# Expert layers in 19 passes of 128 places, in an order made on the chip, summed by one-hot products

## The reference, cut to what matters

```python
e_flat = expert_id.reshape(-1)                     # 512 tokens x 2 experts of one group of 8
order = jnp.argsort(e_flat)                        # assignments sorted by expert, 64 experts
...
def expert_block(args):                            # xb (128, 1024); w1, w3 (1024, 256); w2 (256, 1024)
    xb, e = args
    return (jax.nn.silu(xb @ w1[e]) * (xb @ w3[e])) @ w2[e]
...
out = jnp.zeros((n_tok, dm), h.dtype).at[tok_sorted].add(
    g_sorted[:, None].astype(h.dtype) * y_disp[dest])
```

## Time and profile before

| | |
|---|---|
| median of 3 runs | 1572.75 us (1572.18 to 1574.54) |
| span of the profiled execution | 1571.5 us |
| PE busy | 1344.6 us, 86% |
| DVE busy | 491.8 us, 31% |
| ACT busy | 295.4 us, 19% |
| POOL busy | 290.5 us, 18% |
| DMA | 472.17 MB, mean 300 GB/s |

### The profile page before, as it was taken

The page is one execution under the profiler, slowest core; times in us unless marked ns, Lnnn a source line. Parts: engine busy times, 40 slices in busy tenths (PEclk is TensorE's granted clock), DMA queues, the critical chain, the costliest instruction groups (busy, mean ns, idle before and its releaser), DMA issues.

```text
span 1571.5 us, 19548 instructions
## 1 busy us (share of the span) xinstructions
PE 1344.6 (86%) x6176; PEld 624.6 (40%) x6176; DVE 491.8 (31%) x1034; ACT 295.4 (19%) x584; POOL 290.5 (18%) x412
## 2 busy tenths in 40 slices
PE   7999998987887878878799899999978878878786
PEld 5555463332332323333464565453323323333332
DVE  7996145211111111112605572253111111111114
ACT  6236111110010010101235642111100100101000
POOL 2104002332222222222000000003322222222220
PEclk9999999999899998999799899999999998999999
DMA  5423845999999999999410307049999999999996
GB/s 211 166 103 131 347 176 220 374 393 405 405 397 404 403 396 412 397 401 380 174 54 1 121 1 294 23 172 389 402 394 404 390 392 403 404 411 404 394 397 276
DMA packets 83427, 472.17 MB, mean 300 GB/s; under 512 B 13953, under 2 KB 16145, under 8 KB 32816
## 3 DMA queue, kind: packets, MB, share of 16 engines
q1 hardware_dynamic: 69792, 445.25, 71.7%
q0 software_dynamic: 11568, 19.90, 3.8%
q10 hardware_dynamic: 2016, 6.34, 1.0%
HBM read 453.54 MB, written 27.39 MB: 306 GB/s over the span
## 4 chain that ended last, share of the span: by engine, by line
PE 42%; SPq 35%; DVE 11%; DMA 6%; issue 5%; ACT 1%; DVEq 0%; POOL 0%; ACTq 0%; POOLq 0%
SPq L1744 23%; PE ps L1534 13%; SPq L1749 12%; PE ps L1554 5%; DMA ring<-in_moe_w 4%; PE ps L442 4%; PE ps L885 3%; PE ps L904 2%; PE ps L315 2%; PE ps L908 2%; PE ps L431 2%; PE ps L391 2%; PE ps L1524 1%; DVE extra L549 1%; DVE x L558 1%
## 5 line engine op out<-in xcount | busy, mean ns | idle before, releaser
L1534 PE MATMUL ps<-ring,region_b 128*64 128x512 f32 x1408 | 348.8, 653 | 78.2 <-issue 51.3
L1534 PEld LDWEIGHTS ps<-ring,region_b 128*64 128x64 f32 x1408 | 118.2, 150 | 305.8 <-issue 267.1
L1671 DVE TENSOR_TENSOR extra<-extra,ps 128x256 f32<-128x256 f32 x64 | 26.9, 421 | 579.8 <-ACT extra L1608 544.9
L1534 PE MATMUL ps<-wbuf,region_b 128*64 128x512 f32 x320 | 159.6, 657 | 40.0 <-DMA region_a<-in_moe_w 22.2
L1554 PE MATMUL ps<-ring,extra 128*64 128x512 f32 x704 | 160.8, 598 | 34.0 <-DVE extra L1677 31.7
L1534 PE MATMUL ps<-region_a,region_b 128*64 128x512 f32 x320 | 159.8, 658 | 0.0
L1478 POOL DMA_INDIRECT region_b<-hrow,icol x120 | 111.4, 928 | 147.9 <-issue 147.9
L1608 ACT ACTIVATE extra<-ps 128x256 f32<-128x256 f32 x64 | 24.5, 383 | 585.3 <-PE ps L1534 551.7
L1490 POOL DMA_INDIRECT ytok<-extra,icol x120 | 106.1, 884 | 152.6 <-issue 152.6
L1684 DVE COPY extra<-ps 128x512 f32<-128x512 f32 x64 | 44.3, 692 | 241.7 <-PE ps L1554 241.6
L1534 PEld LDWEIGHTS ps<-wbuf,region_b 128*64 128x64 f32 x320 | 46.6, 150 | 145.7 <-issue 136.9
(11 more groups left out here) (322 smaller groups left out, 1511.8 us busy)
## 6 DMA issues: line engine op xcount, KB each, us to landing
ring<-in_moe_w SPq DMA_DIRECT2D x264, 1024.0 KB
wbuf<-in_moe_w SPq DMA_DIRECT2D x80, 1024.0 KB
region_a<-in_moe_w SPq DMA_DIRECT2D x40, 1024.0 KB
ytok<-ring SPq DMA_DIRECT2D x8, 1024.0 KB, 10.2
wbuf<-in_ev_w_in SPq DMA_DIRECT2D x3, 2048.0 KB, 14.3
wbuf<-in_ev_w_out SPq DMA_DIRECT2D x2, 2048.0 KB, 14.6
hrow<-region_a ACTq DMA_DIRECT2D x8, 512.0 KB, 10.4
region_a<-ytok SPq DMA_DIRECT2D x8, 512.0 KB, 5.0
```

Source lines behind the costliest of these rows:

```text
L1534: last = TE.matmul(ps[CAP * g:CAP * (g + 1), 2 + j, :], xtr[j][:, k, CAP * g:CAP * (g + 1)], up_weights(2 * slot + g, k), start=k == 0, st ...
```

## The change

The 64 experts are put in an order made on the chip. Experts 0 to 5 come first as they are. Of the others, those with more than 32 assignments are put on the eight further wide places, and the rest follows (`turns`). CAP is 32: a block has 128 places and holds either two wide experts of 64 or four of 32 (`strips`). There are 19 blocks or passes, in the order `ORDER`: two, two, four, and then four times two, four, four, four experts. DVE also makes the list `elist` of experts by turn, and SP reads each expert's number from it before it loads its weights. The six slots are now slots of single experts. Each pass has one gather of 128 places.

In a pass of four, up and down products are for four strips of 32 columns. Nothing is scattered: `pick` makes for each pass a one-hot matrix with the gates, and `te_combine` multiplies it with `yo` in eight products of 128 by 128 by 512, which DVE adds into x; `ytok`, its zeros and its read-back are gone. `hid`, `hidT`, `yo` and the up product's bank are there once. The sixth slot's up weights lie in `extra` in place of `region_a`, and all six first experts are loaded ahead of the first up product; what `extra` held in the expert layers is in a new buffer, `scr`. The overflow blocks compute with 32 places for an expert.

```diff
-CAP = 64
-QUART = CAP // 4
+CAP = 32
+ROWS = 4 * CAP
+HEAVY = 8
+STATIC = 6
 OVMAX = 2 * T // CAP - 1
-NBLK = NE + OVMAX + 1
...
+def strips(block):
+    if block < 2:
+        return [(64 * g, 64, 2 * block + g) for g in range(2)]
+    if block < 6:
+        return [(64 * g, 64, 2 * block + 2 + g) for g in range(2)]
+    if block == 6:
+        return [(32 * g, 32, r) for g, r in enumerate((4, 5, 14, 15))]
+    return [(32 * g, 32, 4 * block - 12 + g) for g in range(4)]
+ORDER = [0, 1, 6] + [b for i in range(4) for b in (2 + i, 7 + 3 * i, 8 + 3 * i, 9 + 3 * i)]
+NP = len(ORDER)
+NBLK = NP
+TIMES = [(p, r) for p, b in enumerate(ORDER) for _, _, r in strips(b)]
+WHEN = {r: t for t, (p, r) in enumerate(TIMES)}
+PASS_AT = [p for p, r in TIMES]
...
-            S.wait_ge(s_zf, 128)
+            S.wait_ge(s_wc, 2)
...
+        def places_tensor(l):
+            for i in range(2):
+                TE.wait_ge(s_hot, 2 * l + i + 1)
+                for j in range(8):
+                    last = TE.matmul(ps[:, 6 - i, 0:NBLK], hot_s[:, j, :], hot_v[i][:, j, :], start=j == 0, stop=j == 7)
+                last.then_inc(s_tab, 1)
+            TE.wait_ge(s_ec, l + 1)
+            TE.matmul(ps[0:1, 7, 0:NE], ecol[0:NE, :], ident[0:NE, 0:NE], start=True, stop=True).then_inc(s_er, 1)
...
+            vlink(V.memset(xin[1], 0.0))
...
+            of_choice(rk8, rk.rearrange("p c (g e) -> p c g e", g=NG))
             V.wait_ge(s_rc, 2 * l + 2)
-            ts(quart, cnt, float(QUART), ALU.is_gt)
-            for j in range(2, CAP // QUART):
-                stt(quart, cnt, float(QUART * j), quart, ALU.is_gt, ALU.add)
-            vlink(V.tensor_copy(used[:, :], quart[0:1, :]))
-            turned_ranks(rk)
-            of_choice(destf, place.rearrange("p c (g e) -> p c g e", g=NG))
...
+        def turns(l):
+            late, row, two = (con[:, i:i + NE] for i in (C_LATE, C_ROW, C_WIDE))
+            stt(e1, cnts, CAP + 0.5, late, ALU.is_gt, ALU.mult)
+            vlink(V.tensor_tensor_scan(e2, ones[:, 0:NE], e1, 0.0, ALU.mult, ALU.add))
+            ts(hn, e2[:, NE - 1:NE], -(STATIC - 1.0), ALU.add)
+            stt(e3, e2, 2.0, tcount[:, 0:NE], ALU.mult, ALU.subtract)
+            stt(e3, e3, hn, e1, ALU.subtract, ALU.mult)
+            stt(e1, e2, e2[:, NE - 1:NE], late, ALU.subtract, ALU.mult)
+            tt(e3, e3, e1, ALU.subtract)
+            tt(turn_of, e3, tcount[:, 0:NE], ALU.add)
+            stt(wide, turn_of, STATIC + HEAVY - 0.5, two, ALU.is_lt, ALU.mult)
+            ts(e1, turn_of, float(STATIC + HEAVY), ALU.min, 32.0, ALU.mult)
+            stt(e1, turn_of, 32.0, e1, ALU.mult, ALU.add)
+            ts(e2, turn_of, STATIC + HEAVY - 0.5, ALU.is_gt, 64.0, ALU.mult)
+            tt(e1, e1, e2, ALU.add)
+            tt(e1, e1, row, ALU.add)
+            stt(e1, wide, 8192.0, e1, ALU.mult, ALU.add)
...
+        def places(l):
+            of_choice(code8, by_expert(e1))
+            ts(wide8, code8, 8191.5, ALU.is_gt)
+            stt(over8, wide8, -float(CAP), rk8, ALU.mult, ALU.add)
+            ts(far8, over8, CAP - 0.5, ALU.is_gt, FAR, ALU.mult)
+            stt(dest8, wide8, -8192.0, code8, ALU.mult, ALU.add)
+            tt(dest8, dest8, rk8, ALU.add)
+            tt(dest8, dest8, far8, ALU.add)
+            ts(blk8, dest8, 1.0 / ROWS, ALU.mult, -(ROWS - 1) / (2.0 * ROWS), ALU.add)
+            ts(blk8, blk8, ROUND, ALU.add)
+            ts(blk8, blk8, -ROUND, ALU.add)
+            stt(dest8, blk8, -float(ROWS), dest8, ALU.mult, ALU.add)
+            tt(hot_b, tcount[:, None, 0:NBLK].to_broadcast([P, 8, NBLK]),
+               blk8[:, :, None].to_broadcast([P, 8, NBLK]), ALU.is_equal)
+            tt(hot_v[0], hot_b, con[:, C_ID8:C_ID8 + 8][:, :, None].to_broadcast([P, 8, NBLK]), ALU.mult)
+            V.tensor_tensor(hot_s, tcount[:, None, 0:ROWS].to_broadcast([P, 8, ROWS]),
+                            dest8[:, :, None].to_broadcast([P, 8, ROWS]), ALU.is_equal).then_inc(s_hot, 1)
...
+        def gated_places(l):
+            V.tensor_tensor(hot_v[1], hot_b, g12[:, :, None].to_broadcast([P, 8, NBLK]), ALU.mult).then_inc(s_hot, 1)
+        def expert_list(l):
+            ts(eqt, turn_of[0:NE, :], con[0:NE, C_PIX:C_PIX + 1], ALU.is_equal)
+            tt(eqt, eqt, tcount[0:NE, 0:NE], ALU.mult)
+            V.reduce_sum(ecol[0:NE, :], eqt, AX.X).then_inc(s_ec, 1)
...
+        def tables_vector(l):
+            V.wait_ge(s_tab, 2 * l + 1)
+            V.tensor_scalar(blkidx[:, :], ps[:, 6, 0:NBLK], float(NOROW), None, ALU.add).then_inc(s_dst, 1)
+            ts(tokf, ps[:, 6, 0:NBLK], float(NOROW), ALU.add)
+            V.wait_ge(s_tab, 2 * l + 2)
+            vlink(V.tensor_copy(gatef, ps[:, 5, 0:NBLK]))
+            V.wait_ge(s_er, l + 1)
+            V.tensor_copy(elist[:, :], ps[0:1, 7, 0:NE]).then_inc(s_el, 1)
...
+            V.tensor_scalar(back.rearrange("p c t -> p (c t)"), tcount, tokf[:, b:b + 1], gatef[:, b:b + 1],
+                            ALU.is_equal, ALU.mult).then_inc(s_sel, 1)
...
-        def ex_scatter(l, p, j):
-            G.wait_ge(ml["s_ye"][l], 2 * p + 2)
-            G.sem_inc(s_gate2, 1)
-            glink_at(G.tensor_copy(icol[0:CAP, 4 + 2 * j:6 + 2 * j], blkidx[0:CAP, 1, bass.ds(2 * p, 2)]), s_ic[l][1], p + 1)
-            def rows(g, n):
-                G.indirect_dma_start(ytok[l],
-                                     bass.IndirectOffsetOnAxis(ap=icol[0:n, 4 + 2 * j + g:5 + 2 * j + g], axis=0),
-                                     yo[j][CAP * g:CAP * g + n, :], None, bounds_check=2 * T - 1, oob_is_err=False)\
-                    .then_inc(s_yst[l][j], 16)
-            for g in range(2):
-                quarters(2 * p + g, g, rows)
...
+        def gather(n):
+            l, q = n // NP, n % NP
+            if q > 1:
+                G.wait_ge(s_xtp, 2 * (n - 1))
+            b = ORDER[q]
+            G.indirect_dma_start(xin[q % 2], None, hrow[l], bass.IndirectOffsetOnAxis(ap=blkidx[:, b:b + 1], axis=0),
+                                 bounds_check=T - 1, oob_is_err=False).then_inc(s_xi[q % 2], 16)
+        def moe_gpsimd(l):
+            G.wait_ge(s_hst, 64 * l + 64)
+            G.wait_ge(s_dst, l + 1)
+            for q in range(1, NP):
+                gather(NP * l + q)
+        def te_rows(n):
...
+                for r, t in strip_slots(q):
+                    last = TE.matmul(ps[r, 2, :], xtr[:, k, r], up_weights(t % SLOTS, k),
+                                     start=k == 0, stop=k == KC - 1)
+            last.then_inc(s_up, 1)
...
+        def te_combine(n):
+            TE.wait_ge(s_ye, 2 * n + 2)
+            TE.wait_ge(s_sel, n + 1)
+            for i in range(8):
+                if 8 * n + i > 3:
+                    TE.wait_ge(s_ca, 8 * n + i - 3)
+                TE.matmul(ps[:, SUMS[i % 4], :], back[:, i // 2, :], yo[:, (i % 2) * 512:(i % 2 + 1) * 512],
+                          start=True, stop=True).then_inc(s_cb, 1)
...
+            te_rows(NP * l)
+            places_tensor(l)
+            for q in range(NP):
+                n = NP * l + q
+                te_up(n)
+                if q < NP - 1:
+                    te_rows(n + 1)
+                te_hidden(n)
+                te_down(n)
+                te_combine(n)
+                if q == NP - 2:
+                    extra_tensor(l, overflow(TE, l))
...
+        def added(n, i):
+            V.wait_ge(s_cb, 8 * n + i + 1)
+            xs = x[:, i // 2, (i % 2) * 512:(i % 2 + 1) * 512]
+            V.tensor_tensor(xs, ps[:, SUMS[i % 4], :], xs, ALU.add).then_inc(s_ca, 1)
...
+            SP.wait_ge(s_el, l + 1)
+            for q in range(NP):
+                todo = []
+                for t in range(STATIC, NE):
+                    if PASS_AT[t] == q:
+                        r = TIMES[t][1]
+                        e = SP.value_load(elist[0:1, r:r + 1], min_val=0, max_val=NE - 1)
+                        todo.append((t, e))
+                for t, e in todo:
+                    SP.wait_ge(s_up, NP * l + PASS_AT[t - SLOTS] + 1)
+                    up_weights_load(t % SLOTS, l, e, s_w13[t % SLOTS])
+                for t, e in todo:
+                    SP.wait_ge(s_dn, 2 * (NP * l + PASS_AT[t - SLOTS]) + 2)
+                    down_weights_load(t % SLOTS, l, e, s_w2[t % SLOTS])
...
-        def combine_sync(l):
-            for j in range(2):
-                nc.sync.wait_ge(s_yst[l][j], 8 * NE - 32 * j)
-            for n in range(8):
-                c, k = n // 2, n % 2
-                nc.sync.dma_start(gath[n // 4][:, n % 4, :], ytok[l][k * T + c * P:k * T + (c + 1) * P, :])\
-                    .then_inc(s_gat[c], 16)
...
-            sp.wait_ge(s_wc, 2)
-            for l in range(2):
-                rows_ = ytok[l].rearrange("(a p b) d -> a p (b d)", p=P, b=2)
-                for n in range(4):
-                    sp.dma_start(rows_[n], toep.rearrange("p s n -> p (s n)")).then_inc(s_zf, 16)
...
+            for e in range(4):
+                up_load(0, e)
```

(47 more changed lines are left out.)

818 lines of the change are left out of this document (318 added, 500 removed).

## The result

The changed kernel takes **1526.97 us** (median of 4 runs, 1526.58 to 1527.47) against 1572.47 (4 runs, 1570.88 to 1574.54): ratio 0.971, 95% interval 0.9696 to 0.9724, faster by 45.5 us. The prediction said 1530. The profiled execution has a span of 1524.8 us.

The account below looks back on a forecast made before the run. The weight stream was taken as the bound, with PE waiting. Start 2.7 plus 495.7 gave 498.4 us a layer, saving 23.2 and 18.9: 1571.5 - 42.1 = 1529.4, as a median 1530.7, said as 1530; eight in ten 1504 to 1562.

Parts of the forecast that it names:

- Gathers, 1.5 us a pass: Weight stream in the expert layers: each pass's 128-place gather costs 1.5 us, low end 0.54, high end 1.98.
- goes with DMAs: Stretch of 4 us at 338 GB/s in each old pair: if its loss follows DMA count, 0.93 us a pass.
- goes with rows: The same stretch of slow weight stream: if its loss follows gathered rows, 1.98 us a pass.
- Start, +2.7 us: Routing ahead of each layer's first up product: DVE's new chain makes it 2.7 us later, range 1 to 6.
- 6 us late: Failure sign: the prediction fails if the first up product starts over 6 us late.
- Holes, 5.8 and 7.6 us and 0.8 later: Early passes: DMA idles 5.8, then 7.6 us, as loads wait for up products of passes 1 and 2; 0.8 in pass 5.
- Four strips abreast, 6.9 and 3.65: Four-expert passes: four 32-column strips run side by side, up product 6.9 us, down product 3.65, as for two experts.
- the prediction's 1.3 times: Four-strip products: by the Trainium skill they would cost about 1.3 times what was taken, for a sum of 1548.
- Stream, 421 GB/s: Weight stream in the expert layers: 3 MiB at 421 GB/s, 7.47 us for each of 58 experts.
- The rival of 398: Weight stream stays at 398 GB/s, slowed by the mix with PE's and DVE's reads: 1560 us, chance 0.12.
- One-hot product, 7.1 with additions beneath it: End of each pass: one-hot product takes 7.1 us, eight additions run beneath it, the last ending 0.8 behind.
- Zeros, 0: First mixer: removing the 8 MB of zeros was taken to save 0 us.

Follow-up runs that it names:

- the pair of runs on the kernel before: The kernel before without its scatters, 1550.52 us, and without its row gathers from the third pair on, 1500.47 us, both against 1572.76.
- a_no_early_sums: The changed kernel without the one-hot products and additions of passes 0 and 1 in each layer: 1505.86 us, ratio 0.9571.

## Why the prediction was right, step by step

The size held, and so did the cause: the stream is the bound, and it is shorter by the scatters and by gathers in fewer DMAs. By the runs the scatters were worth 22.2 us, and the gathers' price went from 72.3 to 28.5; the longer starts (13.1) and the holes (some 20) take half of these 66 us back. By its own ledger (1529.4 predicted for the span, 1524.8 measured) errors of opposite sign nearly cancel: the starts came 7.7 us longer in sum, the layers behind them 11.3 shorter. That the number is so close is in part luck.

**Gathers, 1.5 us a pass.** Mis-sized: 1.0. The choice of the middle between "goes with DMAs" (0.93) and "goes with rows" (1.98) was the error; the runs say DMAs. The prediction's working with 1.0 gives 489.2 a layer for its 495.7, 6.5 less. The reading of the earlier trace rows behind it, that the slow stretch is the gather's and not the scatter's, is shown by the pair of runs on the kernel before.

**Start, +2.7 us.** Mis-sized, and the step that failed is the sentence that PE's table products end inside DVE's chain. From the first record of the rows product to the first up product were 12.8 us (234.07 to 246.87), and are now 19.4 (235.77 to 255.16), 19.7 in layer 1: +6.6 (in layer 1, from 13.3, +6.5), past the 6 us late at which the prediction said that it would fail; only the other terms kept the sum. Before, the rows product and the one table, of 16 records:

```profile
234.07 7.03 PE L1280 MATMUL ps<-region_a,extra 128*128 128x512 f32 x16
241.52 1.89 PE L1295 MATMUL ps<-extra 128*64 128x64 f32 x16 [0.41 <-DVE extra L1381]
```

After, DVE's copy of the rows, and the rows product, the tables and the first up product of layer 1:

```profile
249.91 0.67 DVE L1644 COPY region_b<-ps 128x512 f32<-128x512 f32 x1
```

```profile
1013.57 7.03 PE L1316 MATMUL ps<-region_a,region_b 128*128 128x512 f32 x16
...
1026.06 7.01 PE L1325 MATMUL ps<-region_b 128*128 128x19 f32 x32 [3.19 <-DVE region_b L1425]
...
1033.31 9.63 PE L1553 MATMUL ps<-ring,region_b 128*64 128x512 f32 x32
```

DVE's chain was costed well (the copy of the rows is through at 250.6). PE was not: the tables wait for DVE's one-hots until 247.9, and 8 products, 16 records, for each of two tables, at 219 ns a record and the lower clock, end at 254.9. Wide weights against 19 moving columns stood in no row that I had read, and I priced neither the shape nor the clock. The kernel before had the nearest row, its own table at 118 ns a record: at that rate (an estimate) 32 records need 3.8 us, and end at 251.7, behind the copy of the rows too.

**Holes, 5.8 and 7.6 us and 0.8 later.** Measured 10.0 in two holes where they were said to be, and shown to lie on the path by `a_no_early_sums`. Most of the 3.4 us less go with passes 0 and 1, which took 23.0 and 22.1 (255.16 to 278.12 to 300.23) for 24.1 and 24.0: the overflow places fit beneath the one-hot product, and the counts held it up by 1.38 us, not 3.0. Passes that wait for nothing take PE 20.5 (300.23 to 320.71), not 21.1.

**What is left over in the layers.** With gathers at 1.0 and holes of 10.0 the working would come to some 485.8 (an estimate: 489.2 less 3.4). The profile has 491.7 and 488.4, so 5.9 and 2.6 us are losses that no term held. In layer 0, 2.2 are in the tail: from the last up product to the last addition 25.9 (720.96 to 746.87) for 23.75, where DVE works on the next norm between additions. About 1.0 is POOL's loads of router weights, named above. The rest is in part a late hole, which both layers have in the last group of passes. In layer 1:

```profile
1440.00:1450.00 10.00, 10.00 (x70) 3.49 (x62) 0.78 (x2) 0.52 (x2) 0.00 (x0) 0.77 0.83 342
```

```profile
1448.94 0.81 SPq L1696 DMA_DIRECT2D wbuf<-in_moe_w  x2
```

SP issues the next loads right behind the up product of that pass, which began after a wait of 3.65 us, took 9.96 and ended at 1448.73: (422 - 342)/422 x 10 = 1.9 us lost. In layer 0 the same pass's product took 9.77, and 670 to 680 ran at 389 GB/s. No run shows what these dips cost by themselves, and what is left beside them stays open.

**Four strips abreast, 6.9 and 3.65.** Held: 7.07 to 7.09 at the full clock, 3.65, and 8.4 to 10.0 after a wait. The prediction said that the longer ones cost nothing in passes with slack. In most passes DMA was the bound anyway, but in the last group their end also holds the slots (the late hole above). The rate from 128 moving columns carried over to 512. The Trainium skill ("TensorE: Matmul & The Clock Gate", "Measured speedup vs the span model") gives 2.38 times for three column tiles and 3.07 for four row tiles, short of 3 and 4. The trace shows no such loss between two and four column strips of float32: 64 records take 7.08 us where 32 take 7.09. What two strips bring over one no run here shows, and the prediction's 1.3 times was set against two strips, not one.

**Stream, 421 GB/s.** 417 to 418 with gathers, 420 without: held. The rival of 398 is out.

**One-hot product, 7.1 with additions beneath it.** 7.13 in every pass read but the second, where DVE's counts held it up by the 1.38 us; the last addition ends 23.4 us after the last up product starts in layer 1 (1498.30 to 1521.72), predicted 8.8 + 2.5 + 3.65 + 0.9 + 7.1 + 0.8 = 23.8.

**Zeros, 0.** Held, within 4 us.

**What no term held.** The second layer's rows product starts 266.7 us after the last addition of the first, against 269.3 before. Most of it lies in the projection that follows. Before, PE entered it at half the clock, behind an idle stretch of 4.07 us ahead of a transpose group, which waited for DVE; that the read-back's end held DVE there is argued and not shown by a run. Before:

```profile
774.00:780.00 6.00, 5.26 (x10) 3.23 (x11) 3.75 (x14) 2.33 (x4) 0.00 (x0) 0.54 0.00 0
```

After:

```profile
752.00:758.00 6.00, 5.17 (x18) 3.34 (x18) 3.64 (x14) 2.39 (x4) 0.00 (x0) 1.00 0.01 3
```

Ten records in those 6 us before, 18 after; from its start to the transposes of line 968 (989 after) the projection needs 21.4 and 19.0 us. The other way, layer 0's first mixer was 1.7 us longer in this execution, inside the scatter named above.

**Sum**, against the prediction: first mixer +1.7, starts +3.9 and +3.8, layers -4.0 and -7.3, second mixer -2.6, behind the last addition -0.1: -4.6, and 1529.4 - 4.6 = 1524.8.

## What to carry to other kernels

Ask of a slow stretch beside a stream which of the DMAs makes it, and whether it goes with DMAs, rows or bytes: here each gather cost half a microsecond of the stream beside its bytes, with 16 rows as with 128 places, so one gather of 128 places beats two of 64. Where the stream becomes the bound, the time moves to its two ends: price the first up product's start and the passes in which slots are still scarce before anything in the middle. A table made by many products of few columns on wide weights is a cost of its own, and so is the clock behind it: here it fell to 0.50 within two such tables.
